# Gated linear attention interleaved with its own input product, its intermediates on the accumulator banks

## The reference, cut to what matters

```python
proj = x @ w_in                                   # q, k, v, g (3072 columns) and 16 columns a1
log_a = log_sigmoid(a1 @ w_a2 + b_a) / 16
b = cumsum(log_a)                                 # within each chunk of 64 tokens
q_dec, k_dec, k_end = q*scale*exp(b), k*exp(-b), k*exp(b_last - b)
att = where(causal, q_dec @ k_dec.T, 0)           # within a chunk
u = k_end.T @ v                                   # one update of the state per chunk
state[n+1] = exp(b_last)[n] * state[n] + u[n]
o = att @ v + q_dec @ state                       # per head
o = o * rsqrt(mean(o*o) + eps) * norm_g * silu(g)
return o @ w_o
```

## Time and profile before

| | |
|---|---|
| median of 3 runs | 1389.72 us (1389.06 to 1389.92) |
| the profiled execution's own time | 1389.7 us |
| its span, first to last instruction | 1388.0 us |
| mean granted TensorE clock | 0.984 |
| PE, DVE, ACT, POOL busy | 96%, 66%, 48%, 2% |
| from the end of the input product's last matmul to the start of the output product's first | 30.66 us (85.11 to 115.77) |

### The profile page before, as it was taken

The page is one execution under the profiler, slowest core; times in us unless marked ns, Lnnn a source line. Parts: engine busy times, 40 slices in busy tenths (PEclk is TensorE's granted clock), DMA queues, the critical chain, the costliest instruction groups (busy, mean ns, idle before and its releaser), DMA issues.

```text
span 1388.0 us, 21763 instructions
## 1 busy us (share of the span) xinstructions
PE 1335.4 (96%) x8748; PEld 1196.3 (86%) x8748; DVE 917.2 (66%) x1089; ACT 667.7 (48%) x764; POOL 26.9 (2%) x52
## 2 busy tenths in 40 slices
PE   7999999999999999997999989999999998999997
PEld 7988888888986888885998879999989987999997
DVE  4645765566355765657566677777786658777775
ACT  5534544445455544445445544444555455444454
POOL 0000000000021000001000000000100000000000
PEclk9989999999999999998999999999999999999999
DMA  9642555553533555552533345555445324555520
GB/s 365 230 142 91 212 190 199 194 197 136 185 112 122 182 182 182 191 198 104 183 132 113 133 171 181 181 181 181 161 151 182 132 91 167 188 181 181 181 91 31
DMA packets 33378, 229.35 MB, mean 165 GB/s; under 512 B 3728, under 2 KB 4112, under 8 KB 5920
## 3 DMA queue, kind: packets, MB, share of 16 engines
q1 hardware_dynamic: 31536, 220.21, 45.3%
q10 hardware_dynamic: 1776, 8.18, 1.6%
HBM read 227.34 MB, written 1.05 MB: 165 GB/s over the span
## 4 chain that ended last, share of the span: by engine, by line
PE 88%; DVE 6%; ACT 3%; issue 2%; DMA 1%; SPq 0%; POOL 0%; ACTq 0%; DVEq 0%
PE ring L333 20%; PE ring L331 10%; PE ring L274 9%; PE ring L275 9%; PE ring L276 9%; PE acc L376 4%; PE acc L378 4%; PE acc L377 4%; PE acc L274 3%; PE acc L276 3%; PE acc L275 3%; PE ring L376 1%; PE ring L378 1%; PE ring L377 1%; ACT whi L258 1%
## 5 line engine op out<-in xcount | busy, mean ns | idle before, releaser
L266 DVE TENSOR_TENSOR wlo<-raw,whi 128x2048 fp32r<-128x2048 f32 x207 | 473.1, 2289 | 185.0 <-ACT whi L258 184.9
L258 ACT CAST whi<-raw 128x2048 fp32r<-128x2048 f32 x207 | 394.0, 1907 | 115.8 <-PE ring L276 49.7
L333 PE MATMUL ring<-xs,whi 128*128 128x512 f32 x1184 | 424.8, 401 | 0.0
L331 PE MATMUL ring<-xs,wlo 128*128 128x256 f32 x1184 | 335.8, 284 | 10.8 <-DVE acc L1269 10.6
L333 PEld LDWEIGHTS ring<-xs,whi 128*128 128x128 f32 x1184 | 224.9, 190 | 54.5
L274 PE MATMUL ring<-xs,whi 128*128 128x256 f32 x832 | 242.8, 292 | 11.9 <-DVE wlo L1474 6.7
L331 PEld LDWEIGHTS ring<-xs,wlo 128*128 128x128 f32 x1184 | 226.2, 191 | 13.3 <-issue 11.2
L275 PE MATMUL ring<-xs,whi 128*128 128x256 f32 x832 | 237.4, 285 | 0.0
L276 PE MATMUL ring<-xs,wlo 128*128 128x256 f32 x832 | 237.4, 285 | 0.0
L274 PEld LDWEIGHTS ring<-xs,whi 128*128 128x128 f32 x832 | 161.8, 194 | 17.2 <-issue 7.1
L275 PEld LDWEIGHTS ring<-xs,whi 128*128 128x128 f32 x832 | 161.8, 195 | 1.1 <-issue 1.0
(11 more groups left out here) (264 smaller groups left out, 1744.0 us busy)
## 6 DMA issues: line engine op xcount, KB each, us to landing
raw<-wstream SPq DMA_DIRECT2D x207, 1024.0 KB, 4.9
sq<-lnp ACTq DMA_DIRECT2D x4, 1024.0 KB, 4.9
cst<-consts ACTq DMA_DIRECT2D x1, 1025.0 KB, 14.9
hT<-xT SPq DMA_DIRECT2D x4, 256.0 KB, 4.9
raw<-wstream SPq DMA_DIRECT2D x4, 256.0 KB, 5.4
hT<-xtok ACTq DMA_DIRECT2D x1, 1024.0 KB, 16.3
misc<-decay ACTq DMA_DIRECT2D x1, 1024.0 KB, 4.9
out<-y SPq DMA_DIRECT2D x4, 256.0 KB, 2.3
```

Of the source, the lines that this page charges most:

```text
L258: act.copy(whi[:, c % SPLIT, :], raw[:, c % RAW, :]).then_inc(hi_made, 1)
L266: dve.tensor_tensor(wlo[:, c % SPLIT, :], raw[:, c % RAW, :], whi[:, c % SPLIT, :].bitcast(f32), ALU.subtract).then_inc(lo_made, 1)
L331: pe.matmul(bank(b + t)[:, 0:256], wl[:, w], xhi[:, k, :], start=k == 0, stop=False, skip_group_check=True)
L333: mm = pe.matmul(bank(b + t), wh[:, w], xs[:, k, :, :].rearrange("p a s -> p (a s)"), start=False, stop=k == NT - 1, skip_group_check=True)
```

## The change

The twelve pieces and the attention are now issued as one sequence. On PE: behind piece 7 the keys are turned and the scores made (`turned_keys`), behind piece 8 the updates n = 0 and 1, now alternating between them for each head (`first_updates`), behind piece 9 the update n = 2 (`last_update`), behind piece 10 the outputs of heads 0 and 1 (`first_outputs`), and behind piece 11 `variance(0)`, `variance(1)`, the outputs of heads 2 and 3, `variance(2)` and `variance(3)`. Keys, scores and updates are written to the banks of `acc` in place of those of `ring`. The instructions themselves are the same, with the same shapes. ACT copies keys and scores behind the evacuation of piece 7 and squares heads 0 and 1 behind that of piece 10, and the rest of its order is rewritten; DVE's splits of pieces 9 to 14 move in among the updates and the scaling.

```diff
@@ PE @@
-            wide_product(C_GLA_IN, 12, FREE["gla_in"], 0, range(4, 8), {0: gate_input, 1: gate_logits})
-            for h in range(GLA_H):
-                pe.wait_ge(g_kend, h + 1)
...
-            pe.wait_ge(g_ktc, 1)
-            keT = two(yf[:, 0:1024])
-            for n in range(3):
-                r = slice(64 * (n % 2), 64 * (n % 2) + 64)
-                if n == 1:
-                    pe.wait_ge(g_attc, 2)
-                if n == 2:
-                    pe.wait_ge(g_st, 1)
...
+            def update(n, h):
+                r = slice(64 * (n % 2), 64 * (n % 2) + 64)
+                return pe.matmul(columns(2 * (n % 2) + h // 2)[:, (h % 2) * 256:(h % 2) * 256 + 256],
+                                 keT[r, n // 2, h * 128:h * 128 + 128], v[r, n // 2, h * 256:h * 256 + 256],
+                                 start=True, stop=True)
+
+            def first_updates():
+                pe.wait_ge(gemm_free, FREE["gla_in"] + 8)
+                pe.wait_ge(g_ktc, 1)
+                pe.wait_ge(g_attc, 2)
                 for h in range(GLA_H):
+                    for n in range(2):
+                        mm = update(n, h)
+                        if h == GLA_H - 1:
+                            mm.then_inc(g_ud, 1)
+
+            def last_update():
+                pe.wait_ge(g_st, 1)
                 for h in range(GLA_H):
+                    mm = update(2, h)
                 mm.then_inc(g_ud, 1)
...
+            def first_outputs():
+                pe.wait_ge(g_attm, 2)
+                pe.wait_ge(g_st, 3)
+                output(0)
+                output(1)
+
+            wide_product(C_GLA_IN, 12, FREE["gla_in"], 0, range(4, 8),
+                         {0: gate_input, 1: gate_logits, 7: turned_keys, 8: first_updates, 9: last_update,
+                          10: first_outputs}, wait_last=False)
+            pe.wait_ge(gemm_free, FREE["gla_in"] + 11)
+            variance(0)
+            pe.wait_ge(gemm_free, FREE["gla_in"] + 12)
+            variance(1)
+            output(2)
+            output(3)
+            variance(2)
+            variance(3)
@@ ACT @@
-            evacuate(C_GLA_IN, 12, gla_dest, {0: a1_copy, 1: gate_ln, 4: gate_exp})
-            load_exp_ln()
...
-            split_hi(act, C_GLA_O + AHEAD)
...
-            for i in range(GLA_H + 3):
-                if i < GLA_H:
-                    squares_of_o(i)
-                if 0 <= i - 1 < GLA_H:
-                    inverse_root_of_o(i - 1)
-                if 0 <= i - 3:
-                    high_of_o(i - 3)
+            evacuate(C_GLA_IN, 12, gla_dest, {0: a1_copy, 1: gate_ln, 4: gate_exp, 7: keys_copied, 10: first_squares})
+            load_exp_ln()
+            inverse_root_of_o(0)
+            inverse_root_of_o(1)
+            high_of_o(0)
+            squares_of_o(2)
+            high_of_o(1)
+            squares_of_o(3)
+            split_hi(act, C_GLA_O + AHEAD)
+            inverse_root_of_o(2)
+            inverse_root_of_o(3)
+            high_of_o(2)
+            high_of_o(3)
@@ DVE @@
-            for c in range(7, 12):
-                split_lo(dve, c + AHEAD)
+            split_lo(dve, 7 + AHEAD)
+            split_lo(dve, 8 + AHEAD)
             for n in range(3):
-                dve.wait_ge(g_ud, n + 1)
+                dve.wait_ge(g_ud, max(n + 1, 2))
...
+                if n == 1:
+                    split_lo(dve, 9 + AHEAD)
+            split_lo(dve, 10 + AHEAD)
+            split_lo(dve, 11 + AHEAD)
             for h in range(GLA_H):
...
                 if h:
                     x_low(1, lambda i: pair(y, i), [h - 1])
+                if h == 1:
+                    split_lo(dve, C_GLA_O + AHEAD)
```

More of the change, by code:

```diff
@@ L596, in gate_logits @@
                 mm.then_inc(gate_done, 1)
-            wide_product(C_GLA_IN, 12, FREE["gla_in"], 0, range(4, 8), {0: gate_input, 1: gate_logits})
-            for h in range(GLA_H):
-                pe.wait_ge(g_kend, h + 1)
-                for t in range(2):
[L602 to L606, removed]
-                for h in range(GLA_H):
-                    mm = pe.matmul(ring[:, 2 + t, h * 128:h * 128 + 128], kT[:, h, tok], qT[:, h, tok],
-                                   start=True, stop=True)
-                mm.then_inc(g_attd, 1)
@@ L611, in _, with columns, turned_keys @@
-            pe.wait_ge(g_ktc, 1)
-            keT = two(yf[:, 0:1024])
-            for n in range(3):
-                r = slice(64 * (n % 2), 64 * (n % 2) + 64)
-                if n == 1:
-                    pe.wait_ge(g_attc, 2)
-                if n == 2:
-                    pe.wait_ge(g_st, 1)
+            def columns(b):
+                return acc_bank(b)
+            def turned_keys():
+                for h in range(GLA_H):
+                    pe.wait_ge(g_kend, h + 1)
+                    for t in range(2):
+                        mm = pe.transpose(columns(t)[:, h * 128:h * 128 + 128], kT[:, 4 + h, t * 128:t * 128 + 128], ident)
+                mm.then_inc(g_ktd, 1)
+                pe.wait_ge(g_dec, 1)
+                for t in range(2):
+                    tok = slice(t * 128, t * 128 + 128)
+                    for h in range(GLA_H):
+                        mm = pe.matmul(columns(2 + t)[:, h * 128:h * 128 + 128], kT[:, h, tok], qT[:, h, tok],
+                                       start=True, stop=True)
+                    mm.then_inc(g_attd, 1)
@@ new lines, in _ @@
+            keT = two(yf[:, 0:1024])
+            attm = two(sqf[:, 1024:2048])
+            def update(n, h):
+                r = slice(64 * (n % 2), 64 * (n % 2) + 64)
+                return pe.matmul(columns(2 * (n % 2) + h // 2)[:, (h % 2) * 256:(h % 2) * 256 + 256],
+                                 keT[r, n // 2, h * 128:h * 128 + 128], v[r, n // 2, h * 256:h * 256 + 256],
+                                 start=True, stop=True)
+            def first_updates():
+                pe.wait_ge(gemm_free, FREE["gla_in"] + 8)
+                pe.wait_ge(g_ktc, 1)
+                pe.wait_ge(g_attc, 2)
+                for h in range(GLA_H):
+                    for n in range(2):
+                        mm = update(n, h)
+                        if h == GLA_H - 1:
+                            mm.then_inc(g_ud, 1)
@@ L626, in _, with output @@
[L626 to L637, removed]
+            def output(h):
                 for e in range(2):
@@ L649, in _, with variance @@
                 mm.then_inc(g_od, 1)
-                if h:
-                    variance(h - 1)
-            variance(GLA_H - 1)
+            def variance(h):
+                pe.wait_ge(g_sq, h + 1)
+                if h >= 2:
+                    pe.wait_ge(g_rs, h - 1)
+                for e in range(2):
+                    mm = pe.matmul(bank(2 + h % 2)[:, 0:256], ones, kT[:, 2 * h + e, :],
+                                   start=(e == 0), stop=(e == 1))
+                mm.then_inc(g_var, 1)
+            def first_outputs():
[14 more added lines that the diff above has]
+            variance(3)
             rows_product(0, C_GLA_O, 1, lambda: pe.wait_ge(g_rs, GLA_H), (0, 1), lambda: wide_half(C_MLP[0], 2, 0))
@@ L1047, in gla_dest, with keys_copied @@
                 return pair(gT, j - 8), ACT.Silu, 1.0
-            evacuate(C_GLA_IN, 12, gla_dest, {0: a1_copy, 1: gate_ln, 4: gate_exp})
-            load_exp_ln()
[L1051 to L1056, removed]
-            split_hi(act, C_GLA_O + AHEAD)
+            def keys_copied():
+                act.wait_ge(g_ktd, 1)
+                own.mark(act.copy(yf[:, 0:512], acc_bank(0)))
+                act.copy(yf[:, 512:1024], acc_bank(1)).then_inc(g_ktc, 1)
+                for t in range(2):
+                    act.wait_ge(g_attd, t + 1)
+                    act.copy(sqf[:, 1024 + t * 512:1536 + t * 512], acc_bank(2 + t)).then_inc(g_attc, 1)
             def squares_of_o(h):
@@ L1070, in high_of_o, with first_squares @@
                 act.copy(pair(xhi, h), pair(y, h)).then_inc(xh_made, 1)
-            for i in range(GLA_H + 3):
-                if i < GLA_H:
-                    squares_of_o(i)
-                if 0 <= i - 1 < GLA_H:
-                    inverse_root_of_o(i - 1)
-                if 0 <= i - 3:
-                    high_of_o(i - 3)
+            def first_squares():
+                squares_of_o(0)
+                squares_of_o(1)
+            evacuate(C_GLA_IN, 12, gla_dest, {0: a1_copy, 1: gate_ln, 4: gate_exp, 7: keys_copied, 10: first_squares})
[11 more added lines that the diff above has]
+            high_of_o(3)
             load_gb(0)
@@ L1510, in _ @@
             dve.tensor_tensor(kf[:, 0:1024], kf[:, 0:1024], sqf[:, 1024:2048], ALU.mult).then_inc(g_dec, 1)
-            for c in range(7, 12):
-                split_lo(dve, c + AHEAD)
+            split_lo(dve, 7 + AHEAD)
+            split_lo(dve, 8 + AHEAD)
             for n in range(3):
-                dve.wait_ge(g_ud, n + 1)
+                dve.wait_ge(g_ud, max(n + 1, 2))
```

(2 more changed lines are left out.)

6 lines of the change are left out of this document (removed).

## The result

| | before | changed |
|---|---|---|
| median | 1389.39 us (1387.75 to 1389.92, 4 runs) | 1376.88 us (1376.09 to 1377.47, 4 runs) |
| profiled execution: span | 1388.0 us | 1375.3 us |
| mean granted clock | 0.984 | 0.989 |

The ratio is 0.991, with a 95% interval from 0.9898 to 0.9923. 1378.9 was forecast, with a range from 1377.6 to 1382.0. The direction and the likeliest case were right, and the saving is 12.5 us where 10.8 was forecast.

What follows compares the result with a forecast made beforehand. PE, busy 96% of the span, was taken as the bound, losing time only to waits and low clock. Terms of 19.6 + 0.2 + 0.15 = 19.95 us replace 30.66, so 1389.7 - 10.8 = 1378.9 us, range 1377.6 to 1382.0.

Steps and rivals of the forecast that it cites:

- the likeliest case: Attention stretch: PE's waits go and its clock stays up, time as summed, 1378.9 us (1377.7 to 1380.2); chance 0.66.
- Everything behind the output product's start moves as a block: After the attention: later splits follow PE's own progress, so the code behind shifts unchanged, with 0 saved there.
- the stretch: From piece 7's copy to the output product's first matmul: 10.75 us less.
- The first updates: Updates n = 0 and 1, alternating between array row halves: 2.4 us, bounds 1.99 and 2.96, against 2.96 before.
- Keys and scores: Attention, from the first transpose to the start of the updates: 2.81 us of PE time.
- the 0.15 for the ties: Tail behind piece 11: 0.15 us added for three near-simultaneous handovers between PE, ACT and DVE.
- going in and out of pieces: Changes between pieces and 64-row groups on PE: 0.2 us more, with 0 and 0.8 as the ends.
- The value of the low clock: Attention before the change: running at half clock costs 5.8 us in all.
- Rival (b): Attention: the clock falls all the same; time 1381 to 1384.7 us, 1382 the likeliest; chance 0.15.
- Rival (c): Tail: bound by the ACT and DVE chain, not PE; time 1380.2 to 1381.2 us; chance 0.16.
- (d): Pieces 12 or 14: PE waits on a late split, making the kernel slower; time 1392 us or more; chance 0.015.
- (e): Tail: waits of 9 us or more come back, so the change does nothing; chance 0.015.

Runs made afterwards that it cites:

- simple shift: Changed kernel with 8, 16 or 28 extra matmuls, results not used, behind the first updates; medians 1377.56, 1379.61 and 1380.61 us.
- second profile of before: Kernel before, no edit, profiled again; median 1389.79 us against 1390.76, ratio 0.9994; profiled span 1383.7 us.
- all behind piece 11: Changed kernel with the whole attention behind piece 11, new banks, alternation and tail's order kept; median 1386.68 us against 1389.68 of before.
- the filled kernel: Kernel before with six extra matmuls of constants, two before update n = 2, four before the last state's wait; median 1383.65 us against 1390.76.
- the outputs' kernel: Changed kernel with outputs of heads 0 and 1 and ACT's squares of them behind piece 11 instead of 10; median 1376.32 us, ratio to before 0.9907.
- start filled: Changed kernel with ten extra matmuls, results not used, ahead of the logits' wait near 24 us; median 1376.80 us.
- far wait filled: Changed kernel with twelve extra matmuls of constants in PE's wait for the norm ending the second MLP; median 1376.09 us, ratio to before 0.9908.

## Why the prediction was wrong

**The step that failed** is "Everything behind the output product's start moves as a block". In order and in instructions it does. But the later stretches at 1.2 GHz do not move with it: the fall at the second MLP's norm came 12.6 us earlier (631.07 for 643.71), where the mark in the code came 10.6 us earlier. So they caught less dense work, and that made the rest 1.1 to 2.4 us shorter in the changed kernel's three profiles than in all four of before's. In the first profile that is 2.34 us less, of which the late start took 0.98 back, so 1.36 us of the 1.9 by which the profiled span fell short of the sum. The sum had nothing for it, and neither had the range, whose lower end came from terms inside the stretch alone. That there are such stretches could be read from before's page: a mean clock of 0.984 over 1388 us is (1 - 0.984) x 2 x 1388 = 44 us at the low level, and the attention has 13.6 of them. The prediction does not count the others.

What sets how far the fall lies ahead of the mark (its lead) is not settled. It is no simple shift (1, 2 and 3.4 us gave 4.8, 5.8 and 6.7 us of lead, and 4.3 us in the second profile of before changed nothing), and not the low clock inside the attention (all behind piece 11 has 13.6 us of it and a rest of 1270.08). Part of it is chance: the same changed kernel gave 5.6, 5.6 and 6.6. That four executions of before agree within 0.3 us is unexplained. That the rest differs where the clock is low, and not where it is high, is what the matmuls' distances show; no run moved the fall on purpose and left all else alone.

**The term that was off** is the stretch: 10.75 forecast, 11.34 measured, and the terms are these. The first updates took 1.93 (71.38 to 73.31) and not 2.4: the two row groups overlap in full, and the true value was below the lower bound of 1.99, since the next matmul starts before the last one's tail has ended. Keys and scores took 2.58 rather than 2.81, the last update 1.92 rather than 1.99. Outputs took 8.8 rather than 8.68, variances 3.76 rather than 3.7, and the 0.15 for the ties was nothing. The four pieces between took 23.5 rather than 23.04, so going in and out of pieces costs 0.5 and not 0.2. Together the work took 0.4 less, and another 0.1 to 0.2 comes from the ends of the stretch. This term alone would have left the time inside the range.

**Right:** the likeliest case, with no wait on PE over 0.1 us and the clock at 2.4 GHz throughout. The value of the low clock, 5.8 us, has its test in the filled kernel: 5.2 us shorter with 0.45 us of extra delay, so some 5.7. The tail's ties are real and cost nothing. Rival (b), a fall in the stretch in spite of the cover, was not seen in any of ten profiles with the pieces as cover. Rival (c) is refuted by the tail without a wait, and by the outputs' kernel, in which the tail is another and the time the same. Rivals (d) and (e) did not occur: DVE's splits were there in time.

The 11.3 us of the stretch, put together: 4.5 of idle time, 5.2 to 5.8 of low clock, 1.0 of alternation; these add to 10.7 to 11.3. And in one execution of before out of four the low clock lasted only 3.4 us, so there the same change is worth 7.3.

None of the variants beats the changed kernel by more than the runs can tell: 1376.09, 1376.32 and 1376.80 beside 1376.88 and 1377.17.

## What to carry to other kernels

Where a short serial part follows a long dense product on the same engine, put its steps between the last pieces of the product, one dependent step per piece. Waits of 0.5 to 2 us are then filled with dense work. About half of the gain in the stretch was TensorE's clock, which had been low for 13.6 us in three of four profiles and stayed up once the waits were filled. For a forecast, add up the low-clock stretches of the whole program and not only those of the changed part: each may catch a microsecond more or less, and the range has to hold that. Alternate matmuls on different halves of the array's rows: sixteen took the time of eight here.

## What the runs showed of the hardware that I had not expected

Filling 2.4 us of waits with useless matmuls made the kernel before 7.1 us faster. Filling a wait of 5.8 us elsewhere gained nothing: the clock fell at the next waits, of 1.5 us or less, and 3.4 us of low time lay on dense work as before.

Near the start the clock fell behind an idle time of 0.35 us, with ten full matmuls before it and eight 16-row matmuls behind it (start filled, 27.7 us), and did not fall in another execution of nearly the same code with an idle time of 1.03 us (far wait filled). Idle time alone doesn't decide it from one execution to the next.

Four executions of one kernel took the same 1272.1 to 1272.2 us for the same part of the program while what lay ahead of it differed by up to 5.9 us (111.46 to 117.39), and three executions of another took 1269.9 to 1271.0 for the same instructions.
